# The state space part of a decoder step in groups of four tokens, and projection and GLU work placed among the first gathers

## The reference, cut to what matters

```python
q, k, v, u = split(x @ w_in + b_in)                  # x: tokens x 1024, w_in: 1024 x 2048
att = merge of three dilated causal windows of q, k, v with ALiBi (8 heads of 64)
# S5: 32 groups of 16 channels, 64 complex states each
h_t = a * h_(t-1) + z * (B u_t);   y_t = Re(C h_t) + D u_t
z = gelu(y);  ssm = z * sigmoid(z @ w_glu + b_glu)
h = LN1(ALPHA * x + concat(rms(att), rms(ssm)) @ w_out + b_out)
# PEER, per token: 8 heads; the 16 best of 128 keys twice, then the 16 best of 256 pairs
e = experts of the token (128 of 16384);  g = softmax(scores)
a = gelu(h . peer_u[e]);  ffn = sum over e of g * a * peer_v[e]
y = LN2(ALPHA * h + ffn + sigmoid(h @ w_ple_gate) * (p @ w_ple))
```

## Time and profile before

| | |
|---|---|
| median of three runs | 1945.04 us |
| the profiled execution's own time | 1951.28 us |
| its span, first to last instruction | 1949.5 us |
| mean granted clock of PE | 0.741 of full |
| first gather issued | 268.18 us |
| busy: PE, DVE, ACT, POOL | 68%, 69%, 41%, 40% |
| gathers | 576, 604.02 MB, 75.5% of the 16 transfer engines' span |
| all transfers | 723.17 MB, 371 GB/s over the span |

### The profile page before, as it was taken

How to read it: one execution, slowest core, us unless ns; L and a number is a source line. 1 busy time by engine, 2 the same in 40 slices (tenths; PEclk the granted TensorE clock), 3 DMA queues, 4 the chain that set the end, 5 groups by cost and what they waited for, 6 DMA issues and landing times.

```text
span 1949.5 us, 23865 instructions
## 1 busy us (share of the span) xinstructions
PE 1326.9 (68%) x7204; PEld 646.9 (33%) x7204; DVE 1350.4 (69%) x3212; ACT 793.6 (41%) x2757; POOL 777.9 (40%) x796
## 2 busy tenths in 40 slices
PE   7999886774764866656664655555746666677876
PEld 6765572331232333324321222122221333322221
DVE  6967898864748779888987753444444467886665
ACT  2132247772424344544543443333333223354554
POOL 0953324443434444455443333233233344444442
PEclk9999996776886677777776677766767555576977
DMA  7012689999999999999999999999999999999997
GB/s 299 1 44 93 200 312 421 397 373 421 411 387 415 352 421 421 421 421 420 417 391 416 421 414 420 420 421 421 422 412 422 421 420 405 412 416 417 413 422 287
DMA packets 101024, 723.17 MB, mean 371 GB/s; under 512 B 12016, under 2 KB 12784, under 8 KB 20784
## 3 DMA queue, kind: packets, MB, share of 16 engines
q0 software_dynamic: 82944, 604.02, 75.5%
q1 hardware_dynamic: 17968, 117.77, 15.4%
HBM read 714.78 MB, written 4.87 MB: 369 GB/s over the span
## 4 chain that ended last, share of the span: by engine, by line
DMA 37%; PE 22%; DVE 13%; ACT 7%; issue 6%; POOL 1%; POOLq 0%; ACTq 0%; DVEq 0%; another core or an unknown queue 0%
DMA R<-d_uv,W 37%; PE bank L1408 8%; DVE R L2169 7%; PE bank L1321 3%; PE bank L1295 3%; PE bank L1162 3%; ACT W L1682 1%; ACT L1679 1%; PE bank L1291 1%; PE bank L1154 1%; ACT W L1687 1%; PE bank L1355 1%; POOL R L919 1%; PE bank L1208 1%; ACT W L1650 1%
## 5 line engine op out<-in xcount | busy, mean ns | idle before, releaser
L919 POOL DMA_INDIRECT R<-d_uv,W x576 | 671.8, 1166 | 1011.1 <-PE bank L1408 832.0
L2169 DVE CUSTOM_DVE_ANT_0 R<-R,W 128x1024 f32<-128x1024 f32 x576 | 696.7, 1223 | 473.1 <-DMA R<-d_uv,W 456.1
L1408 PE MATMUL bank<-R,W 128*32 128x512 f32 x2296 | 473.4, 848 | 558.9 <-ACT W L1687 550.5
L1650 ACT CAST W<-W 128x2 uint32<-128x2 f32 x292 | 55.7, 192 | 883.5 <-DVE W L2169 866.8
L1408 PEld LDWEIGHTS bank<-R,W 128*32 128x32 f32 x2296 | 81.6, 125 | 798.5 <-ACT W L1687 724.6
L1687 ACT ACTIVATE W<-W 128x32 f32<-128x32 f32 x576 | 153.5, 313 | 9.7
L1682 ACT ACTIVATE W<-W 128x1 f32<-128x1 f32 x576 | 138.2, 287 | 9.7
L1321 PEld LDWEIGHTS bank<-E 128*128 128x128 f32 x864 | 123.7, 230 | 35.7 <-issue 35.7
L1321 PE MATMUL bank<-E 128*128 128x128 f32 (+1 forms) x864 | 129.7, 317 | 0.5 <-issue 0.5
L963 PE MATMUL bank<-E,W 128*128 128x256 f32 (+1 forms) x384 | 102.9, 427 | 10.1 <-DMA E<-d_xT 7.9
L963 PEld LDWEIGHTS bank<-E,W 128*128 128x128 f32 x384 | 75.4, 200 | 31.5 <-issue 10.1
(11 more groups left out here) (334 smaller groups left out, 1807.9 us busy)
## 6 DMA issues: line engine op xcount, KB each, us to landing
E<-d_kc SPq DMA_DIRECT2D x8, 2560.0 KB
E<-d_w_pq SPq DMA_DIRECT2D x6, 2048.0 KB, 12.7
E<-d_vc SPq DMA_DIRECT2D x8, 1536.0 KB, 26.2
R<-d_uv,W POOLq DMA_INDIRECT x576
E<-d_w_out SPq DMA_DIRECT2D x4, 2048.0 KB, 12.7
E<-d_vc SPq DMA_DIRECT2D x8, 1024.0 KB, 30.5
W<-d_w_in SPq DMA_DIRECT2D x3, 2048.0 KB, 21.1
W<-d_w_pq SPq DMA_DIRECT2D x3, 2048.0 KB, 8.2
```

The lines of the kernel that those rows point to most:

```text
L919: pool.indirect_dma_start(ring[r], None, A["uv"], bass.IndirectOffsetOnAxis(ap=stage[:, half, s:s + 1], axis=0),).then_inc(landed[r], 16)
L1408: last = mm(acc(half, TG * column_group(js[s], half), TG), wsel[:, r, :], ring[r][:, D + half * 512:D + half * 512 + 512], start=False, st ...
L1650: return nc.scalar.copy(stage[:, half, PAIR * x:PAIR * x + PAIR], egall[:, 0, at])
L2169: last = nc.vector.tensor_tensor_reduce(ring[r][:, 0:D], ring[r][:, 0:D], hrep[:, js[s], :], 1.0, 0.0, ALU.mult, ALU.add, dots[:, x, s:s + 1])
```

## The change: groups of four tokens, and the order around the first gathers

The tokens of a block are laid out in group order (first the 32 tokens at place 0 of their group, then those at place 1, and so on). This holds for x, k, v and the mask, and the host puts k and v back in order at the end. The S5 part then has four steps instead of sixteen, one for each channel quarter, and each does all 512 tokens: 128 groups of four.

- u is made in pieces of 128 channels in which the four places of a group stand on four sets of 32 rows (512 matmuls of 32 weight columns and 128 tokens), and the sample tokens' u in a piece of its own (`us`).
- `Bt`, the input weights times the powers of a, is built on the chip: three rounds of six operations on DVE, 32 transposes on PE (`turn_b`), and copies on ACT. `make_c` builds the output weights times the powers of a (five rounds of six on DVE). `kernel_of` makes the small matrix on PE (four times 48 matmuls of 32 columns) and ACT copies it into `T`.
- `ssm_in` is 8 matmuls of 128 rows for each quarter, `ssm_out` 12 of them, and `z_turn` brings the result back to channels on rows (16 matmuls of 32 columns). POOL takes only the last state, and does the sample tokens' recurrence after the fourth scan. `match_out(0, 0)` waits for its end (`sx_ready`).
- The second part of q is made in the front. The second part of k is made around the first gather, from a part of w_in that is loaded a second time (`w_again`, 2 MB). v of blocks 2, 3 and 4 is made at pairs 0, 2 and 4, and GLU of blocks 1, 2 and 3 at pairs 3, 6 and 7. The rest of attention begins at pair 9 instead of 1, with two units every one and a half pairs.
- `ask(0, 2)` and `ask(0, 3)` move from the end of the front to pairs 11 and 18. The first gathers find four free slots (`free(0)`), two more after k's last piece, and two more after `ask(0, 1)`.
- Of the mask, the first block's 512 KB come early, and the whole 2 MB again after the last GLU block. SP's loads of `w_pq` 1, 2 and 3 and the stores of k and v stand at other places.

The first matmuls of the program on PE, before. `W` holds weights, `E` activations, `bank` is an accumulator, and xN is how many in a row (here one entry is one matmul).

```diff
+SUB = 4
+CHUNKS = SEQ // SUB
...
-PIECES = ([("u", c, x) for x in range(2) for c in range(CT)] + [(kind, c, 0) for kind in "qk" for c in range(CT)]
-          + [("v", 0, 0)] + [(kind, c, 1) for kind in "qk" for c in range(CT)] + [("v", b, 0) for b in range(1, BLOCKS)])
-FIRST_V = 4 * CT
...
+PIECES = ([("u", c, 0) for c in range(CT - 1)] + [("us", 0, 0), ("u", CT - 1, 0)] + [(kind, c, 0) for kind in "kq" for c in range(CT)]
+          + [("v", 0, 0)] + [("q", c, 1) for c in range(CT)] + [("v", 1, 0)] + [("k", c, 1) for c in range(CT)]
+          + [("v", b, 0) for b in range(2, BLOCKS)])
...
 def order_of_front():
...
-    steps = 4 * QB
-    pieces = {n: [2 * CT + 2 * n, 2 * CT + 2 * n + 1] for n in range(9)}
...
-    order += [("free", 5, 0), ("ask", 0, 2, 0), ("ask", 0, 2, 1), ("free", 1, 2), ("ask_out", 0, 2)]
-    order += [("ask", 0, 3, 0), ("ask", 0, 3, 1), ("free", 2, 3),
...
+    order += [("tm", 0), ("ssm_in", 0)] + piece("us", 0, 0) + [("s_in",)] + piece("u", 3, 0)
+    order += [("scan", 0), ("ssm_in", 1), ("tm", 1), ("make_c",)]
+    order += [x for c in range(CT) for x in piece("k", c, 0)] + [x for c in range(2) for x in piece("q", c, 0)]
...
+    order += [("normal", 0, 0), ("normal", 0, 1), ("turn", 0), ("turn_out", 0), ("ask", 0, 0, 0), ("ask", 0, 0, 1)]
+    order += [("ask_out", 0, 0), ("match", 0, 0), ("match_out", 0, 0), ("s_ssm_out",), ("free", 0)]
+    order += [("tops", 0, 0, j) for j in range(4)] + piece("k", 0, 1) + piece("k", 1, 1)
+    order += [("cross", 0, 0, 0), ("cross", 0, 0, 1), ("resolve", 0, 0, 0), ("resolve", 0, 0, 1)] + piece("k", 2, 1)
+    order += [("s_skip_term",), ("lay", 0, 0, 0), ("lay_too", 0, 0, 1), ("first_stage",), ("alpha",)] + piece("k", 3, 1)
+    order += [("free", 1), ("ask", 0, 1, 0), ("ask", 0, 1, 1), ("free", 2), ("ask_out", 0, 1), ("match", 0, 1), ("match_out", 0, 1)]
...
-ATT_AT = 1
-GLU_AT = 7
-PROJECT_AT = 35
+ATT_AT = 9
+PROJECT_AT = 36
...
+        at[glu].append(("glu_block", b))
+        at[gate].append(("gate_block", b))
+        at[product].append(("product_rest", b))
+        at[product + 1].append(("sums_rest", b))
...
-    pick(1, 0, 0, 0, 0, 0, 1, 2, 3, 4, 5)
-    pick(2, *range(6, 22, 2), 22, 23)
-    pick(3, *range(24, 40, 2), 40, 41)
+    pick(1, 1, 2, 3, 4, 5, 6, 7, 8, 9, 10)
+    look(11, 2)
...
-            load(xT[0], A["xT0"], in_x[0])
+            load(xT[:, 0:2], A["xT0"], in_x[0])
+            load(xT[:, 2:4], A["xT1"], in_x[1])
...
+            sp.wait_ge(bu_full, CT)
+            load(pbias_first, A["pbias"][:, :, SEQ - P:SEQ], in_pb_first)
+            sp.wait_ge(hs_ready, CT)
+            load(wout_first[1], eight(A["w_out"][1]), in_out[1])
+            sp.wait_ge(y_full, CT)
+            load(glu, A["glu"], in_glu)
+            load(w_again, eight(A["w_in"][1]), in_w[1])
+            sp.wait_ge(carried, CT)
+            sp.dma_start(A["stp_out"], sm[:, 14:16, :]).then_inc(outs, 16)
...
+            sp.wait_ge(at_full, 1)
+            sp.wait_ge(at_squared, 1)
+            load(parts_of[0][0], eight(A["w_pq"][0]), in_pq[0])
...
+            sp.wait_ge(sy_full, 1)
+            load(fold, A["fold"], in_fold)
             sp.wait_ge(pq_full, 1)
-            load_early(2)
-            sp.wait_ge(carried, 4 * QB)
...
+            load(parts_of[0][1], eight(A["w_pq"][1]), in_pq[1])
...
+            store_v(0)
+            store_v(1)
+            wait_put(sp, number("k", CT - 1, 1))
+            sp.dma_start(A["k_out"][:, :, 0:SEQ], kT).then_inc(kv_left, 16)
+            sp.dma_start(A["k_out"][:, :, SEQ:TOK], kS).then_inc(kv_left, 16)
+            sp.wait_ge(sy_used, 1)
+            sp.wait_ge(glu_full, QB)
+            load(pbias, A["pbias"], in_pb)
+            sp.wait_ge(proj_full, len(PIECES))
+            load(parts_of[0][2], eight(A["w_pq"][2]), in_pq[2])
+            for b in range(2, BLOCKS):
+                store_v(b)
+            sp.wait_ge(pq_full, 3)
             load(parts_of[0][3], eight(A["w_pq"][3]), in_pq[3])
-            sp.wait_ge(glu_full, QB)
...
-            sp.wait_ge(pq_full, 2)
+            sp.wait_ge(pq_full, 4)
             load(parts_of[1][0], eight(A["w_pq"][0]), in_pq[0])
...
+            def piece_u(c):
...
+                for j in range(4):
+                    for k in range(DC):
+                        for step in range(SUB):
+                            o = bank[32 * step:32 * step + 32, c, j * P:j * P + P].rearrange("p (a b) -> p a b", a=QB)
+                            last = mm(o, w_u(c)[:, k, 32 * j:32 * j + 32], xT_by_step[:, :, k, step, :],
+                                      start=(k == 0), stop=(k == DC - 1), skip_group_check=True)
+                last.then_inc(proj_full, 1)
...
+            def turn_b(g):
...
+                    j, x = 2 * g + n // 2, n % 2
+                    last = nc.tensor.transpose(bank[:, 4 + g % 4, n * P:n * P + P],
+                                               X[:, j, x].rearrange("p a b -> p (a b)"), ident[:, :])
+                last.then_inc(bt_full, 1)
...
+            def kernel_of(q):
...
+                for j in range(4):
+                    for x in range(2):
+                        for step in range(SUB):
+                            r = slice(32 * step, 32 * step + 32)
+                            mm(bank[r, 4, j * P:j * P + 32 * (SUB - step)], Bs[:, 4 * q + j, x, :],
+                               C[:, 4 * q + j, x, 0:SUB - step, :].rearrange("p a b -> p (a b)"),
+                               start=(x == 0), stop=False, skip_group_check=True)
+                    for step in range(SUB):
+                        r = slice(32 * step, 32 * step + 32)
+                        last = mm(bank[r, 4, j * P:j * P + 32], ident[:, r], eyes[:, 4 * q + j, :],
+                                  start=False, stop=True, skip_group_check=True)
+                last.then_inc(k_full, 1)
...
+            def ssm_in(q):
...
-                for x in range(2):
-                    j = (step + x) % 4
-                    r = slice(32 * j, 32 * j + 32)
-                    last = mm(bank[:, 6 + x, j * P:j * P + P], Bt[r, q, x, :], uT[r, q, b * P:b * P + P],
-                              start=True, stop=True)
...
+            def ssm_out(q):
...
+                for j in range(4):
+                    mm(bank[:, 5, j * P:j * P + P], T[:, 4 * q + j, :], ut[:, 4 * q + j, :], start=True, stop=False,
+                       skip_group_check=True)
+                    if j == 0:
+                        pe.wait_ge(hs_ready, q + 1)
+                    for x in range(2):
+                        last = mm(bank[:, 5, j * P + 1:j * P + P],
+                                  C[:, 4 * q + j, x, 1:SUB + 1, :].rearrange("p a b -> p (a b)"),
+                                  H[:, x, j, 0:CHUNKS - 1], start=False, stop=(x == 1), skip_group_check=True)
+                last.then_inc(y_full, 1)
...
+            def z_turn(q):
...
+                for step in range(SUB):
                     for j in range(4):
-                        t = 4 * q + j
-                        c = Csc[:, t, x // 2, :]
-                        last = mm(bank[32 * j:32 * j + 32, 5, 0:P], c, turned[n % 2][x][:, j, :],
-                                  start=(x == 0), stop=(x == 3), skip_group_check=True)
...
+            def free(n):
+                if n == 0:
+                    pe.wait_ge(out_full, 1)
+                    pe.wait_ge(at_squared, 1)
+                elif n == 1:
+                    pe.wait_ge(proj_full, number("k", CT - 1, 1) + 1)
+                else:
+                    pe.wait_ge(pq_full, 2)
+                pe.sem_inc(slot_free, HALF if n == 0 else PAIR)
...
+            def put_b(g):
...
+                nc.scalar.copy(Bt[:, 2 * g:2 * g + 2].rearrange("p a b c -> p (a b c)"), bank[:, 4 + g % 4, :]).then_inc(
+                    bt_put, 1)
...
+            def put_t(q):
...
+                    last = nc.scalar.copy(T[r, 4 * q:4 * q + 4, 32 * step:P], src[r, :, 0:P - 32 * step])
...
+            def gelu(q):
...
+                f(zt.rearrange("p a b -> p (a b)"), bank[:, 5, :], ACT.Gelu_apprx_tanh).then_inc(y_used, 1)
...
+            def z_turn(q):
...
+                nc.scalar.copy(uT[:, q, :].rearrange("p (c t) -> p t c", t=SUB),
+                               bank[:, 4, :].rearrange("p (t c) -> p t c", t=SUB)).then_inc(z_ready, 1)
...
+            for step in range(SUB - 2, -1, -1):
+                re, im = X[:, :, 0, step + 1, :], X[:, :, 1, step + 1, :]
+                tt(c4[0], re, wide(0, 32), ALU.mult)
+                tt(c4[1], im, wide(1, 32), ALU.mult)
+                tt(c4[2], im, wide(0, 32), ALU.mult)
+                link(tt(c4[3], re, wide(1, 32), ALU.mult))
+                tt(X[:, :, 0, step, :], c4[0], c4[1], ALU.add)
+                last = tt(X[:, :, 1, step, :], c4[2], c4[3], ALU.subtract)
...
+            def make_c():
...
+                for d in range(SUB + 1):
...
+                    tt(C[:, :, 0, d, :], c4[0], c4[1], ALU.subtract)
```

(7 more changed lines are left out.)

826 lines of the change are left out of this document (448 added, 378 removed).

## The result

The changed kernel takes 2003.1 us as the median of four runs (2001.56 to 2008.78), beside 1947.3 us for the kernel before in the same comparison. The ratio is 1.0288, with a 95% interval from 1.0255 to 1.0322. The forecast was 1956 us in a range of 1930 to 1977. I had added 11 us to the kernel before and 56 came, about five times as much, and the time lies outside the range. The profiled execution took 2003.27 us, with a span of 2001.5 us at a mean clock of 0.741.

A forecast was written before the change was run, and what follows sets the result against it. PE was taken to bound the front before the first gather, and transferred bytes the rest. -18 + 22 + 5 = +9, with another +2: +11 on 1951.3, so 1962, or 1956 by the median; range 1930 to 1977.

The forecast's parts named there:

- Term 1: Front up to the first gather, priced by PE work and waits: first gather at 250, 18 us earlier.
- the slow stretches: Front: PE at its lower rate in two stretches, at the start and after the transposes, costing 6.6 us.
- Rival B: Front much shorter: waits covered, no slow stretch, first gather at 225 to 235, time 1932; chance 0.23.
- The transposes: Front: 32 transposes at 0.246 us each, 7.9 us; by the skill's rule the first gather up to 15 us later.
- Term 2: Bytes moved from before the first gather to after it: 9.04 MB, +22 us, lower bound 11.
- rival C: After the first gather: moved transfers fall into holes that were there anyway, -5 us, so 1940; chance 0.14.
- Term 3: New holes in the transfers among the gathers, from busy PE and ACT: +5 us, between 0 and +30.
- rival D: PE or ACT jams between 250 and 420 us, holes near +30: +34 us, so 1979; chance 0.16.
- The direction: Whole kernel: slower, by +11 us on the profiled execution's 1951.3.
- my own terms for the rest: After the first gather: +5 us for new holes, +2 because the ring fills a little later.

The follow-up runs named there:

- e12: The repaired kernel: the changed kernel with attention at two pairs for two units, and bias and exps one pair later; 1950.3 us, ratio 0.9997.
- e1: The changed kernel with attention at two pairs for two units instead of one and a half, block's end one pair earlier; 1984.2 us, ratio 1.0179.
- e2: The kernel before with only the changed kernel's attention schedule (start at pair 9, one and a half pairs, closer stages); 2012.2 us, ratio 1.0335.
- e10: The kernel before with the closer attention stages alone, its two pairs kept, started at pair 5; 2004.4 us, ratio 1.0275.
- e18: The kernel before with exps and transposes at pair 2 of a unit instead of 3; 1952.2 us, ratio 1.0018.

## Why the prediction was wrong, step by step

- **Term 1, the front: right in direction, 9 us too timid.** The gain is 27 us against 18. PE was busy for 181.5 us up to the end of the first `match` at 218.27, and I had 182. u's 512 matmuls took 35.0 us against 34.6. PE sat idle for 36.8 us of the 218.27: 10.6 for x at the start, 7.2 for the residual and 19 in pieces of 4 us and less. Without the start that is 26.2, against the 26.6 that I had put down. So the sum without the slow stretches, 243.3, was nearly met, and the 6.6 that I laid on top for them make most of the miss. Slow stretches did come: 64 of u's matmuls took 3.70 us at a clock of 1.00, and the next 64 took 5.36 at 0.72. But u's 35.0 us already hold them; at 3.70 for 64 all of u would be 29.6, so the row that I priced u by had room for them. In part the match of 181.5 with 182 is luck: the transposes took 4.0 us less than I had put down for them, and other parts about as much more. Rival B's condition, a first gather before 246, was met, and the front did not decide the time.

```profile
PE bank L957 <- DMA E<-d_xT: 10.6, 1, 10.6
PE bank L1365 <- DVE E L2335: 7.2, 1, 7.2
PE bank L957 <- issue: 3.9, 4, 2.2
PE bank L1037 <- ACT R L1602: 3.8, 2, 1.9
...
20.30:25.00 4.70, 3.70 (x128) 3.43 (x128) 4.62 (x8) 1.14 (x4) 0.00 (x0) 1.00 1.00 417
26.20:32.40 6.20, 5.36 (x128) 5.05 (x128) 5.86 (x38) 0.00 (x0) 0.00 (x0) 0.72 1.02 431
```

- **The transposes.** 32 in a row took 3.90 us, 0.122 each, half of what I took from the earlier trace rows, where eight stood behind a wait. The granted clock tells why: 1.00 here, 0.50 for the eight in the changed kernel's `turn` at 204 us, which are again 1.97. The S5 input behind the 32 took 2.02 us at 1.00. The rule of the Trainium skill that I had weighed ("TensorE: Matmul & The Clock Gate", section "Part 4: PE-mode transpose") is that transposes do not count as activity for the clock gate. By it the S5 input would have run at half rate; this trace does not show that behind 3.9 us of transposes.

```profile
41.04:48.20 7.16, 5.78 (x50) 5.31 (x50) 7.02 (x16) 5.03 (x12) 0.00 (x0) 1.00 0.01 2
...
204.00:207.00 3.00, 1.97 (x8) 1.57 (x8) 0.02 (x1) 0.91 (x1) 0.00 (x0) 0.50 0.56 124
```

- **Term 2, bytes: over-sized.** I took +22 for 9.04 MB and named 11 as the lower end. Cutting 7.3 MB was worth 6 us with the jam and 5 without it, so as bytes the moved loads mostly fell into holes, as rival C says. C's time, 1940, did not come, since it had no jam. What I left out is that a late load is also waited for: the mask held DVE for 12.0 us in the changed kernel.
- **Term 3, holes: this is the step that failed.** I wrote +5 within 0 to +30, and priced attention by how busy ACT is: 7.6 us of work in 7.5 us of gathers. That is a question of throughput. What decided was a distance: which result of PE another engine asks for, and how many pairs after PE was told to make it. My rival D had the place and the sign, and took the price from ACT's work again, as 1 us for each of 12 steps and as much again for PE. The runs put 53 us on the schedule of attention (changed kernel against e12): 31 (37 by the ratios) on bias and exps standing too close behind PE's scores and transposes, with the wait for the mask in it, and 21 on the spacing, whose mechanism stays open. The order showed the distances before any run: bias and transposes of neighbouring units in the same pair. I had read the new stages and spacing and compared them only with busy times.
- **The direction was luck.** With the front and the bytes at what the runs gave them, and my own terms for the rest, the sum would have been -27 + 6 + 5 + 2 = -14 us, a faster kernel. An over-sized term 2 stood in for a term 3 that was about ten times too small.
- **What the 79 us among the gathers consist of.** 53 (by the medians) to 57 (by the ratios) the schedule of attention; 5 the moved bytes; 6 v and GLU; together some 65. About 11 to 15 us stay open. By the count of gathers the repaired kernel is already behind the kernel before after 109 us (36 issued, against 44) and stays 10 behind after 459 us (154 against 164), so most of them lie in the first thirty pairs, where the later queries, the mask and k's store now stand too. I did not separate these.

## What to carry to other kernels

When work for several in-order engines is interleaved by hand with a pipeline, write down for every wait how many slots lie between the making and the asking, and compare it with how far the asking engine runs ahead. Here PE results that DVE asked for after one pair or none went with an emptied ring in four kernels (changed, e1, e2 and e10), and moving two numbers in a table was worth 31 to 37 us, more than the 27 of the whole restructured front. It is a place to look and not a law: in the kernel before, DVE waits for transposes one pair old too, under transfers that run at 97% to 101%, and asking for them a pair later (e18) gained nothing. If all engines are half idle and the transfers too, look for such a ring in the waits before looking for too much work.

## What the runs showed of the hardware that I had not expected

Eight transposes behind a wait of 7.2 us took 0.246 us each at a granted clock of 0.50, and 32 behind dense matmuls 0.122 each at 1.00. A row measured behind a wait may be at the lower of the two clocks, and then it overstates the same operation elsewhere by two.
